# Late tokens in two and then four token tiles, v rows 140 slots behind the u rows

## The chip, the cores and the metric

One NeuronCore of a Trainium2 chip runs the whole kernel. The metric is the device time of one execution in microseconds, as the median of the runs. Everything is fp32. PE is the matmul engine, DVE the vector engine, ACT the scalar engine, POOL the engine that issues the indirect gathers, and SP the one whose queue issues the other DMAs.

## The reference, cut to what matters

One decoder layer over 1024 tokens of width 1024:

```
a = rms_norm(x, g);  z = a @ w_in                # 1024 x 4864: 38 column tiles of 128
z_rwkv, z_conv, z_gate = split(z)                # 14, 8 and 16 column tiles
z_rwkv = z_rwkv + (token_shift(z_rwkv) - z_rwkv) * mu
o_r = rwkv7(z_rwkv);  o_c = conformer_conv(z_conv)
h = x + (g_r * o_r + g_c * o_c) @ w_out          # g = sigmoid(z_gate)
c = rms_norm(h);  q = c @ w_q;  idx, gate = product_key_top16(q)    # 8 heads x 16 = 128 experts a token
coef = gate * gelu(sum_d(c * u_tab[idx]))        # u: 128 rows of 4 KB for each token
h = h + sum_e(coef * v_tab[idx])                 # v: 128 rows of 4 KB for each token
h = h + sigmoid(rms_norm(h) @ w_ple) * (p @ w_proj);  out = rms_norm(h)
```

For 1024 tokens the u rows and the v rows are 0.54 GB each. Each is read once.

## The kernel before

The tokens are eight tiles of 128 (`NT = 8`). Every engine runs a program written out by hand over positions (t, s): period t, slot s, with 128 slots in a period. In slot s of period t, DVE takes the dot product of c with the u row that expert column s gathered for the 128 tokens of tile t (`dot`). Also in period t each engine does, at fixed slots, its steps of `front` of tile t+1: the RWKV recurrence in slots 20 to 65, the convolution, the mixer products in slots 74 to 84, the query product and the top-k. So the order of the work is fixed on every engine, and an instruction that waits holds all that stands behind it on its engine.

**v rows.** `LAG = 2`: the v rows of tile t-2 are gathered and multiplied in period t. PE adds a gathered row, weighted, with four matmul records into `acc`. The u rows use five buffers (`UR`), the last of them `a_rstd`, and the v rows six (`VR`); once all u rows are done, the v rows use all eleven. POOL issues v row and u row in turn; a gather into a used buffer waits until that buffer's row has been used (`s_dot`, `s_vmm`). Periods 0 and 1 gather u rows alone, 2 to 7 both kinds, 8 and 9 v rows alone.

**The input projection.** The first 256 tokens are projected before period 0 (line 1170). The other 768 go in two blocks of 384 (`BEHIND_T`), one in period 0 and one in period 1 (line 1196): 38 column tiles of 8 products in each, at most four products in a slot, into the two halves of `acc`. A column tile's weights (512 KB) come into one of three buffers. ACT (lines 1411 to 1419) and DVE (`behind_out`) take it out of PSUM into one of two output buffers, halves of `e_hh`, and SP stores it to DRAM (`behind_store`), from where later periods read z, the convolution's input and the gates. The second block's normed x waits in DRAM and is read back at the start of period 1.

**The mixer weights** come through a ring of eight buffers of 256 KB, four of their own and four in `zb`, loaded from slots 40 and 66 on. `e_x` holds x of the next tile from slot 2 on; `e_hh` holds h of the tile whose v rows are being added.

**The end.** `tail` of a tile (the per-layer input gate, the last norm) runs in 20 slots; five tails run in period 7, one each in periods 8 and 9, and the last after them.

Of the kernel before, what the change touches and what calls it, by code (L numbers as in the profile page):

```python
# [122 lines left out]
UR, UW, VR, RING, RINGS = 5, 4, 6, 4, 8  # L123
# [17 lines left out]
AHEAD_T, BEHIND_T, BLOCKS = 2 * P, 3 * P, 2  # L141
W_Q_FIRST = (AHEAD_T + BEHIND_T) // P
# [7 lines left out]
LAG = 2  # L150
# [16 lines left out]
def v_place(m):  # L167

    alone = (NT - LAG) * NSEL
    if m < alone:  # L170
        return m % VR, m // VR + 1
    i, k = (m - alone) % (VR + UR), (m - alone) // (VR + UR) + 1
    return i, (alone // VR + k if i < VR else k)


def v_user(m):

    alone = (NT - LAG) * NSEL
    if m < alone:
        return m - VR if m >= VR else None  # L180
    if m - alone >= VR + UR:
        return m - VR - UR
    return m - VR if m - alone < VR else None
# [71 lines left out]
def block_of(n):  # L255

    return (n * P - AHEAD_T) // BEHIND_T if n * P >= AHEAD_T else None
# [7 lines left out]
def behind_weight(t, s):  # L265

    if not BEHIND_AT[t] <= s < BEHIND_END:
        return 0
    return 1 if HEAVY[0] <= s < HEAVY[1] and not FILLED[0] <= s < FILLED[1] else 3
# [8 lines left out]
def behind_products(t, s):  # L278

    done, total = (sum(behind_weight(t, i) for i in range(n)) for n in (s, SLOTS))  # L280
    first = 0 if t else AHEAD_COLS * KT
    n = COL_TILES * KT - first
    return range(first + n * done // total, first + n * (done + behind_weight(t, s)) // total)
# [7 lines left out]
def ring_slot(n, k):  # L291

    if k < RING:
        return 40 + k
    if k < RINGS:
        return MIX_AT + k - RING if n else FRONT_SLOTS
    return product_slot(k - RINGS)
# [13 lines left out]
def behind_done(t, s):  # L311

    if t == 0 and s < AHEAD_COLS:
        return [s]
    return [i // KT for i in behind_products(t, s) if i % KT == KT - 1]


def tail_step(t, s):

    if t == NT - 1:  # L320
        m, k = divmod(s - TAIL_AT, TAIL_SPAN)
        return (m, k) if 0 <= m < EARLY_TAILS else None
    if NT <= t < NT + LAG and 10 <= s < 10 + TAIL_SPAN:
        return EARLY_TAILS + t - NT, s - 10
    if t == NT + LAG and s < TAIL_SPAN:
        return NT - 1, s
    return None


def trunk(nc, io, dram):  # L330

    with ExitStack() as ctx:
# [15 lines left out]
        ring = [buf(f"e_ring{i}", [P, PAIRS, P]) for i in range(RING)]  # L348
# [3 lines left out]
        ring += [flat_zb[:, i * PAIRS * P:(i + 1) * PAIRS * P].rearrange("p (i t) -> p i t", i=PAIRS) for i in range(RINGS - RING)]  # L352
# [11 lines left out]
        z_r, z_k, z_v, lora = (zin[:, a:b, :] for a, b in ((0, 4), (4, 8), (8, 12), (12, 14)))  # L364
        p_w, p_run, p_dec, p_a = (part(a, 4, "p (i t) -> p i t", i=PAIRS) for a in (14, 18, 22, 26))
# [21 lines left out]
        blocks_at = KT * AHEAD_T  # L387
        behind = v_all[:, 0:3, :].rearrange("p a d -> p (a d)").rearrange("p (k t) -> p k t", k=KT)
        late = flat_q[:, blocks_at:blocks_at + KT * BEHIND_T].rearrange("p (k t) -> p k t", k=KT)
        w_a = [u[i][:, :].rearrange("p (k c) -> p k c", k=KT) for i in range(UW)]  # L390
        w_b = [v[3 + i].rearrange("p (k c) -> p k c", k=KT) for i in range(BW)]
        taken = blocks_at + KT * BEHIND_T
# [9 lines left out]
        b_zs, b_zq = wd[0][:, 0:BEHIND_T + 1], wd[1][:, 0:BEHIND_T]  # L402
        omm = buf("e_omm", [P, RWKV_TILES])
        b_cg = b_zq
        b_zo = [hh[:, i * HALF:i * HALF + BEHIND_T] for i in range(2)]
        z_last = buf("e_z_last", [P, RWKV_TILES])
        a_sq = [hh, gt]
        b_sum = a_rstd[:, AHEAD_T:]
        first_gates = [gt, hh]
# [24 lines left out]
        ps = psum("e_ps", [P, 2, HALF])  # L434
        c = psum("e_c", [P, D])
        pi = pd[:, :].rearrange("p (b t) -> p b t", b=2)
        idx_px, coef_px = ps[:, 0, 2 * NKEY:2 * NKEY + P], ps[:, 1, 2 * NKEY:2 * NKEY + P]

        s_const, s_iota = sem("e_constants"), sem("e_iota_made")
        s_w_q, s_w_tail = [sem(f"e_query_weights_in{i}") for i in range(2)], sem("e_tail_weights_in")  # L440
# [5 lines left out]
        s_late, s_lin = sem("b_late_tokens_stored"), [sem(f"b_late_tokens_in{i}") for i in range(PIECES)]  # L446
# [7 lines left out]
        s_bg = sem("b_mixer_gate_ready")  # L454
        s_bo, s_bst, s_wz = sem("b_output_ready"), [sem(f"b_output_stored{i}") for i in range(2)], sem("e_weights_cleared")
# [22 lines left out]
        s_u = [sem(f"e_u_in{i}") for i in range(UR)]  # L478
        s_v = [sem(f"e_v_in{i}") for i in range(VR + UR)]
# [20 lines left out]
        def tail_h(m):  # L500
            return hh if m == NT - 1 else xin

        @block.sync
        def _(sp):
            def stored(n, m):

                b, outs = block_of(n), stores_until(m)
                if b is None:
                    for i in range(2):
                        sp.wait_ge(s_ast[i], 16 * min(outs, outputs_until(COL_TILES)) // 2)  # L510
                    if outs > outputs_until(COL_TILES):
                        for i in range(2):
                            sp.wait_ge(s_agst[i], 16 * (outs - outputs_until(COL_TILES)) // 2)
                else:
                    for i in range(2):
                        sp.wait_ge(s_bst[i], 16 * (b * stores_until(COL_TILES) + outs) // 2)

            def rec_load(n):
                sp.wait_ge(s_y, n)
                stored(n, RWKV_TILES)  # L520
# [16 lines left out]
            def ring_load(n, which, m):  # L537
# [3 lines left out]
                elif k >= RING:  # L541
                    sp.wait_ge(s_rp, REC_PE * 2 * (n + 1))
                elif n:
                    sp.wait_ge(s_wu, 2 * KT * (n - 1) + k + RINGS + 1)
# [3 lines left out]
            def x_load(n):  # L548
                if n:
                    sp.wait_ge(s_sq, n)  # L550
                    sp.wait_ge(s_ctr, n)
                    sp.wait_ge(s_hout, 16 * n)
                sp.dma_start(xin[:, :], io["x"][n]).then_inc(s_xin, 16)
# [5 lines left out]
            def sum_load(n):  # L559
                sp.wait_ge(s_hout, 16 * (n + 1))  # L560
                if n:
                    sp.wait_ge(s_h2, 16 * n)
                else:
                    for i in range(2):
                        sp.wait_ge(s_bst[i], 16 * BLOCKS * stores_until(COL_TILES) // 2)
# [6 lines left out]
            def tail_loads(m):  # L572
                if m < NT - 1:
                    if m == 0:
                        sp.wait_ge(s_sq, NT)
                        sp.wait_ge(s_ctr, NT)
                        sp.wait_ge(s_hout, 16 * NT)
# [3 lines left out]
                    sp.dma_start(xin[:, :], dram["h2"][m]).then_inc(s_tin, 16)  # L581
# [14 lines left out]
            def front(n, s):  # L596
                if s == 2:
                    x_load(n)
# [10 lines left out]
                if s == MIX_AT + 14 and n + 1 < NT:  # L609
# [15 lines left out]
            def behind_w(b, m):  # L625
                i = b * COL_TILES + m
                if i >= BW:
                    sp.wait_ge(s_bm, i - BW + 1)
                sp.dma_start(w_b[i % BW], io["w_in"][column(m)]).then_inc(s_bw[i % BW], 16)

            def behind_store(b, m):
                i = stores_until(m)
                if kind(m) == "gate":
                    sp.wait_ge(s_bg, b * GATE_TILES + i + 1 - outputs_until(COL_TILES))
# [1546 lines left out]
```

## Time and profile before

| | us |
|---|---|
| median of 3 runs | 3628.08 (3624.88 to 3631.03) |
| span of the profiled execution, first to last instruction | 3429.3 |
| busy PE / DVE / POOL / ACT | 2702.1 / 2374.2 / 1976.9 / 525.9 |
| bytes moved, mean rate | 1249.58 MB, 364 GB/s |

The profiled execution's own device time is not recorded; its span is 198.8 us short of the median of the runs, and that difference is what lies around the span (launch, first loads of the program, end). A busy PE counts the modelled time of its matmuls, also where two run side by side. In the views of stretches each engine has its busy time and, in brackets, its instructions; PEclk is the granted TensorE clock as a share of 2.4 GHz (0.50 is 1.2 GHz); the DMA share can stand a little over 1.

### The profile page before, as it was taken

What the parts mean: (1) busy time and instruction counts of PE and PEld (TensorE: products, weight loads), DVE (VectorE), ACT (ScalarE), POOL (GpSimd) and SP (SyncE); (2) the same over time, 40 slices, a digit from 0 to 9 for tenths busy, and PEclk for the clock granted to TensorE, in tenths of its full rate; (3) what the DMA queues carried; (4) which work ended last, traced back from release to release, by engine and by line L of the source; (5) the groups of instructions that cost most, each with busy time, mean ns of one, the idle gap of its engine ahead of it and who ended that gap; (6) DMA issues with size and microseconds to landing.
All of it is one profiled execution on the core that took longest, in us unless ns stands there. A gap on an engine that the chain in (4) does not pass through costs nothing.

```text
span 3429.3 us, 41510 instructions
## 1 busy us (share of the span) xinstructions
PE 2702.1 (79%) x15300; PEld 1231.4 (36%) x15300; DVE 2374.2 (69%) x6064; ACT 525.9 (15%) x1165; POOL 1976.9 (58%) x2093
## 2 busy tenths in 40 slices
PE   9998998899766777787767767686777767778887
PEld 7775665565422322332233323232333112111111
DVE  5569888979898679877987798769875667520000
ACT  3223122212201011101110011002110111110001
POOL 1003344334577677767676767676766667757663
PEclk9999999999889987888798879887888789789999
DMA  6548899889999999999999999999999999999995
GB/s 211 184 156 284 297 354 335 283 288 344 361 400 406 401 409 409 407 394 406 407 408 401 397 407 408 405 395 409 408 404 404 409 407 407 409 369 393 401 362 237
DMA packets 380043, 1249.58 MB, mean 364 GB/s; under 512 B 40256, under 2 KB 76352, under 8 KB 379072
## 3 DMA queue, kind: packets, MB, share of 16 engines
q0 software_dynamic: 294912, 1073.87, 80.6%
q1 hardware_dynamic: 82624, 172.00, 14.2%
q8 instruction: 121, 1.98, 0.2%
q10 hardware_dynamic: 2304, 1.05, 0.1%
q14 instruction: 82, 0.67, 0.1%
HBM read 1217.27 MB, written 29.49 MB: 364 GB/s over the span
## 4 chain that ended last, share of the span: by engine, by line
DMA 27%; PE 13%; POOL 11%; DVE 10%; issue 5%; ACT 1%; SPq 0%; ACTq 0%; POOLq 0%
DMA e_u<-in_u_tab,e_idx 12%; DMA e_v<-in_v_tab,e_idxT 8%; POOL e_v L806 5%; PE e_acc L1126 5%; DMA e_a_rstd<-in_u_tab,e_idx 4%; POOL e_u L789 4%; DVE e_u L1972 3%; PE e_pd L1090 3%; PE e_pd L1011 2%; DMA e_u<-in_v_tab,e_idxT 1%; DMA e_x<-h_after_experts 1%; POOL e_a_rstd L789 1%; DVE e_a_rstd L1972 1%; DVE e_gbc L1709 1%; PE e_pd L928 1%
## 5 line engine op out<-in xcount | busy, mean ns | idle before, releaser
L1126 PE MATMUL e_acc<-e_v,e_wd 128*32 128x512 f32 x3636 | 1093.3, 719 | 463.6 <-DMA e_v<-in_v_tab,e_idxT 460.1
L789 POOL DMA_INDIRECT e_u<-in_u_tab,e_idx x820 | 797.5, 973 | 859.9 <-DVE e_dots L1972 487.1
L1972 DVE CUSTOM_DVE_ANT_0 e_u<-e_u,e_c 128x1024 f32<-128x1024 f32 x820 | 996.3, 1215 | 379.0 <-DMA e_u<-in_u_tab,e_idx 370.4
L806 POOL DMA_INDIRECT e_v<-in_v_tab,e_idxT x909 | 863.1, 950 | 334.2 <-issue 221.9
L1126 PEld LDWEIGHTS e_acc<-e_v,e_wd 128*32 128x32 f32 x3636 | 146.3, 116 | 1086.9 <-DMA e_v<-in_v_tab,e_idxT 901.6
L1196 PE MATMUL e_acc<-e_v 128*128 128x384 f32 x1216 | 435.5, 503 | 12.7 <-ACT e_wd L1413 11.2
L1972 DVE CUSTOM_DVE_ANT_0 e_a_rstd<-e_a_rstd,e_c 128x1024 f32<-128x1024 f32 x204 | 247.8, 1215 | 91.4 <-DMA e_a_rstd<-in_u_tab,e_idx 91.0
L1709 DVE SCALAR_TENSOR_TENSOR e_gbc<-e_hc,e_cw,e_gbc 128x128 f32<-128x128 f32 x960 | 307.8, 343 | 1.0
L789 POOL DMA_INDIRECT e_a_rstd<-in_u_tab,e_idx x204 | 198.6, 974 | 154.0 <-DVE e_dots L1972 123.9
L1196 PEld LDWEIGHTS e_acc<-e_v 128*128 128x128 f32 x1216 | 227.1, 195 | 162.8 <-issue 39.2
L831 PE MATMUL e_pd<-e_arena 64*64 64x64 f32 x3584 | 149.7, 233 | 52.0 <-DVE e_arena L1612 36.9
L1981 DVE TENSOR_TENSOR e_hh<-e_hh,e_acc 64x512 f32<-64x512 f32 (+1 forms) x24 | 16.4, 682 | 249.7 <-PE e_acc L1126 249.2
L831 PEld LDWEIGHTS e_pd<-e_arena 64*64 64x64 f32 x3584 | 127.0, 144 | 169.3 <-issue 74.1
L1260 ACT ACTIVATE e_arena<-e_pd 128x512 f32<-128x512 f32 (+1 forms) x192 | 90.4, 471 | 566.7 <-PE e_pd L831 373.7
L1011 PE MATMUL e_pd<-e_w_out,e_actT 128*128 128x512 f32 x256 | 134.1, 654 | 20.1 <-DVE e_actT L1846 20.1
L1170 PE MATMUL e_acc<-e_w_q,e_u 128*128 128x256 f32 x608 | 140.3, 386 | 3.4 <-DVE e_w_q L2057 3.4
L1037 PEld LDWEIGHTS e_pd<-e_actT,e_w_q 128*128 128x128 f32 x1024 | 126.4, 200 | 42.9 <-issue 37.5
L1037 PE MATMUL e_pd<-e_actT,e_w_q 128*128 128x128 f32 x1024 | 134.8, 288 | 0.3 <-ACT e_actT L1308 0.3
L1126 PE MATMUL e_acc<-e_u,e_wd 128*32 128x512 f32 x368 | 120.1, 602 | 18.2 <-DMA e_u<-in_v_tab,e_idxT 17.2
L1090 PE MATMUL e_pd<-e_w_out,e_actT 128*128 128x512 f32 x256 | 124.0, 618 | 2.3 <-ACT e_actT L1308 2.3
L1170 PEld LDWEIGHTS e_acc<-e_w_q,e_u 128*128 128x128 f32 x608 | 114.5, 192 | 21.7 <-issue 5.2
L806 POOL DMA_INDIRECT e_u<-in_v_tab,e_idxT x92 | 86.5, 940 | 46.4 <-issue 23.3
(272 smaller groups left out, 2695.3 us busy)
## 6 DMA issues: line engine op xcount, KB each, us to landing
e_v<-in_w_in SPq DMA_DIRECT2D x76, 512.0 KB, 6.3
e_u<-in_w_in SPq DMA_DIRECT2D x38, 512.0 KB, 3.8
e_v<-in_v_tab,e_idxT POOLq DMA_INDIRECT x909, 9.2
e_u<-in_u_tab,e_idx POOLq DMA_INDIRECT x820
e_ring<-in_w_c SPq DMA_DIRECT2D x32, 256.0 KB, 10.6
e_zb<-in_w_c SPq DMA_DIRECT2D x32, 256.0 KB, 7.7
e_ring<-in_w_r SPq DMA_DIRECT2D x32, 256.0 KB, 6.5
e_zb<-in_w_r SPq DMA_DIRECT2D x32, 256.0 KB, 8.1
```

What stands on the lines that cost most here:

```text
L789: pool.indirect_dma_start(out=u[m % UR][:, :], out_offset=None, in_=io["u_tab"], in_offset=bass.IndirectOffsetOnAxis(ap=idx[n % 2][:, j:j ...
L806: pool.indirect_dma_start(out=v[i], out_offset=None, in_=io["v_tab"], in_offset=bass.IndirectOffsetOnAxis(ap=idxT[n % (LAG + 1)][:, k:k + ...
L831: last = pe.matmul(pi[r, out, i * CH:(i + 1) * CH], a[r, i, :], b[r, i, :] if len(b.shape) == 3 else b[r, :], start=True, stop=True)
L1011: last = pe.matmul(pd[:, h * HALF:(h + 1) * HALF], mixt[:, k, :], w_out[:, k, h * HALF:(h + 1) * HALF], start=(k == 0), stop=(k == KT - 1))
L1037: last = pe.matmul(pd[:, h * P:(h + 1) * P], w_q[:, k, h * P:(h + 1) * P], actT[:, k, :], start=(k == 0), stop=(k == KT - 1))
L1090: last = pe.matmul(pd[:, h * HALF:(h + 1) * HALF], actT[:, k, :], w_ple[:, k, h * HALF:(h + 1) * HALF], start=(k == 0), stop=(k == KT - 1))
L1126: last = pe.matmul(acc[rows, cols], w[:, at_:at_ + 32], v[v_place(m)[0]][:, cols], start=(step == 0), stop=True, skip_group_check=True)
L1170: last = pe.matmul(out, w_a[m % UW][:, k, :], ahead[:, k, :], start=(k == 0), stop=(k == KT - 1))
L1196: last = pe.matmul(acc[:, m % 2 * HALF:m % 2 * HALF + BEHIND_T], w_b[n % BW][:, k, :], behind[:, k, :], start=(k == 0), stop=(k == KT - 1))
L1260: act.activation(dst, src, ACT.Copy).then_inc(s_ra, 1)
L1709: dve.scalar_tensor_tensor(out=out, in0=hc[:, i, j:j + P], scalar=col(cw, j * CONV_TILES + i), in1=out, op0=ALU.mult, op1=ALU.add).then_in ...
L1972: dve.tensor_tensor_reduce(u[m % UR][:, :], u[m % UR][:, :], c[:, :], 1.0, 0.0, ALU.mult, ALU.add, dots[n % 2][:, j:j + 1]).then_inc(s_dot, 1)
```

## The change

- Periods 0 and 1: the block of period 0 is now 256 tokens (two tiles). The other 512 tokens (four tiles) are a block of their own in slots 130 to 300, counted from the start of period 0 (period 1 and the first 45 slots of period 2), with two or three products of 512 tokens in a slot and none in the slots of the mixer products.
- The late block has one PSUM bank of its own, `pl`, one weight buffer in two halves of 256 KB (4 of 8 products each), and one pair `l_zs`, `l_zo` in a new buffer `side`. Its x stays in SBUF, in four buffers that later hold rows.
- v rows follow the u rows by 140 slots (`V_LAG`), not by 256. The u rows have 4 buffers and the v rows 4 until slot 312; then 6 and 7; after the last u row the v rows have all 13.
- The mixer weights' ring has 12 buffers, all in memory of the recurrence, all loaded from slot 66 of a period on. `hh` and `xin` are one buffer; `x_load` moves to slot 30, `sum_load` to slot 112. Six tails run in period 7.

```diff
-UR, UW, VR, RING, RINGS = 5, 4, 6, 4, 8
+UW, VW, LW, RINGS = 4, 5, 4, 12
-AHEAD_T, BEHIND_T, BLOCKS = 2 * P, 3 * P, 2
+AHEAD_T, BEHIND_T, LATE_T = 2 * P, 2 * P, 4 * P
-BEHIND_AT, BEHIND_END, PIECES = (2, 4), 124, 4
+BEHIND_AT, BEHIND_END = 2, 120
-LAG = 2
+V_HEAD = 12
+LAG, V_LAG = 1, NSEL + V_HEAD
+CHUNKS = 2
+MORE_AT = 2 * SLOTS + 56
+U_FIRST, V_FIRST = list(range(UW)), list(range(UW, UW + VW - 1))
+U_LATER = U_FIRST + [UW + VW, UW + VW + 1]
+V_LATER = V_FIRST + [UW + VW - 1, UW + VW + 2, UW + VW + 3]
...
+def late_room(s):
+    if HEAVY[0] <= s < FILLED[0] or FILLED[1] <= s < MIX_AT + 32 or MIX_AT + 38 <= s < MIX_AT + 48:
+        return 0
+    return 3 if 10 <= s < REC_AT or s >= MIX_AT + 48 else 2
+def late_slots():
+    at_, g, i = {}, SLOTS + 2, 0
+    first = g
+    while i < COL_TILES * KT:
+        room = late_room(g % SLOTS) if g >= first else 0
+        n = min(room, KT - i % KT)
+        at_[g] = range(i, i + n)
+        i += n
+        if n and i % KT == 0:
+            first = g + 1
+        g += 1
+    return at_
...
             def ring_load(n, which, m):
                 k = which * KT + m
                 if k >= RINGS:
                     sp.wait_ge(s_wu, 2 * KT * n + k - RINGS + 1)
-                elif k >= RING:
+                else:
                     sp.wait_ge(s_rp, REC_PE * 2 * (n + 1))
+                if k == RINGS - 1:
+                    sp.wait_ge(s_rv, REC_DVE * 2 * (n + 1))
...
+            def late_w(q):                                            # SP
+                m, half = divmod(q, CHUNKS)
+                if q >= CHUNKS:
+                    sp.wait_ge(s_lu, q - CHUNKS + 1)
+                sp.dma_start(w_late[:, half, :, :], io["w_in"][column(m)][:, k, :]).then_inc(s_lw[half], 16)
...
+                    for q in late_chunks_done(t, s):                  # SP, in slot s
+                        if q + CHUNKS < CHUNKS * COL_TILES:
+                            late_w(q + CHUNKS)
+                    for m in late_done(t, s, 2):
+                        if kind(m) != "conv gate":
+                            late_store(m)
...
+            def late_product(i):                                      # PE
+                m, k = divmod(i, KT)
+                half, in_half = divmod(k, KT // 2)
+                if k == 0 and m:
+                    pe.wait_ge(s_lf, m)
+                if in_half == 0:
+                    pe.wait_ge(s_lw[half], 16 * (m + 1))
+                last = pe.matmul(pl[:, :], w_late[:, half, in_half, :], late[:, k, :], start=(k == 0), stop=(k == KT - 1))
+                if in_half == KT // 2 - 1:
+                    last.then_inc(s_lu, 1)
...
+            def late_out(m):                                          # ACT; DVE adds l_zs to l_zo a slot later
+                act.wait_ge(s_lu, CHUNKS * (m + 1))
+                i = stores_until(m)
+                    act.wait_ge(s_lst, 16 * i)
+                if kind(m) == "z":
+                    act.activation(l_zs[:, 0:1], col(z_last, column(m)), ACT.Copy)
+                    act.activation(l_zs[:, 1:], pl[:, :], ACT.Copy, scale=col(vec, COL["mu"] + column(m)))
+                    act.activation(l_zo, pl[:, :], ACT.Copy, scale=col(omm, column(m))).then_inc(s_lf, 1)
+                if kind(m) == "gate":
+                    act.activation(l_zo, pl[:, :], ACT.Sigmoid).then_inc(s_lf, 1)
```

## Rows read from the trace of the kernel before

**Rows 1.** Stretches by period: engines' busy time, clock, DMA share, GB/s.
```profile
core 0: us, PE busy (x) PEld busy (x) DVE busy (x) ACT busy (x) POOL busy (x), PEclk, DMA share, GB/s
0.00:257.00 257.00, 239.17 (x1749) 195.17 (x1749) 148.59 (x415) 67.39 (x155) 10.24 (x45) 0.99 0.55 183
257.00:578.00 321.00, 291.56 (x1700) 185.28 (x1699) 281.18 (x742) 73.75 (x151) 126.18 (x131) 0.95 0.91 315
578.00:905.00 327.00, 302.05 (x1732) 192.56 (x1733) 287.23 (x750) 77.95 (x161) 124.57 (x130) 0.96 0.91 311
905.00:1261.00 356.00, 257.16 (x1637) 102.61 (x1636) 283.30 (x730) 43.56 (x101) 251.33 (x262) 0.85 1.02 403
...
2687.00:3023.00 336.00, 247.47 (x770) 64.67 (x770) 217.40 (x506) 50.34 (x111) 237.46 (x249) 0.81 1.03 408
3023.00:3205.00 182.00, 149.93 (x550) 31.97 (x549) 12.44 (x21) 14.38 (x37) 120.38 (x128) 0.97 0.98 383
3205.00:3390.00 185.00, 154.12 (x572) 33.25 (x571) 6.42 (x10) 10.69 (x31) 120.46 (x128) 0.98 0.98 383
```

**Rows 2.** Stretches inside period 1 (slots 0-7, 40-47) and period 3 (slots 0-7).
```profile
580.00:605.00 25.00, 22.41 (x80) 14.27 (x81) 24.83 (x56) 12.96 (x27) 7.93 (x8) 0.85 0.91 331
...
715.00:739.00 24.00, 24.00 (x218) 14.87 (x217) 18.29 (x53) 3.63 (x7) 7.97 (x9) 1.00 0.85 280
...
1263.00:1291.00 28.00, 15.94 (x66) 5.62 (x65) 24.52 (x55) 10.44 (x21) 16.81 (x17) 0.81 1.03 409
```

**Rows 3.** Waits (total, times, longest, us): periods 2 to 6.
```profile
PE e_acc L1126 <- DMA e_v<-in_v_tab,e_idxT: 372.3, 316, 8.8
...
DVE e_u L1972 <- DMA e_u<-in_u_tab,e_idx: 284.3, 305, 8.8
```

**Rows 4.** Waits: period 0.
```profile
POOL e_u L789 <- DVE e_dots L1972: 159.8, 98, 5.9
...
DVE e_u L1972 <- DMA e_u<-in_u_tab,e_idx: 6.7, 6, 1.7
```

**Rows 5.** Timeline of PE: start, us, group; 256, 384 and 512 columns, one v row.
```profile
109.03 1.99 PE L1170 MATMUL e_acc<-e_w_q,e_u 128*128 128x256 f32 x8
...
678.30 4.14 PE L1196 MATMUL e_acc<-e_v 128*128 128x384 f32 x12
...
1003.20 1.05 PE L1126 MATMUL e_acc<-e_v,e_wd 128*32 128x512 f32 x4
...
3064.68 7.13 PE L1090 MATMUL e_pd<-e_w_out,e_actT 128*128 128x512 f32 x16
```

**Rows 6.** Groups of PE (busy, mean ns, idle before), periods 1 and 2.
```profile
L1196 PE MATMUL e_acc<-e_v 128*128 128x384 f32 x608 | 217.5, 503 | 7.4 <-ACT e_wd L1413 6.6 <-ACT e_hh L1419 0.7
...
L1126 PE MATMUL e_acc<-e_v,e_wd 128*32 128x512 f32 x512 | 154.1, 733 | 73.3 <-DMA e_v<-in_v_tab,e_idxT 73.0
```

**Rows 7.** DMA of period 1: queue's share; issues with KB and us to landing.
```profile
q1 hardware_dynamic: 22439, 34.98, 32.1%
...
mixer_gates<-e_hh SPq DMA_DIRECT2D x17, 192.0 KB, 5.5
shifted_projection<-e_hh SPq DMA_DIRECT2D x14, 192.0 KB, 7.8
```

**Rows 8.** DMA of period 2, the same.
```profile
q1 hardware_dynamic: 3692, 8.04, 6.1%
...
e_zb<-in_w_c SPq DMA_DIRECT2D x4, 256.0 KB, 7.7
```

**Rows 9.** DMA of period 0: its gate stores.
```profile
mixer_gates<-e_hh SPq DMA_DIRECT2D x15, 192.0 KB, 9.1
```

**Rows 10.** Groups of ACT by shape: copies out of PSUM, a table load.
```profile
L1260 ACT ACTIVATE e_arena<-e_pd 128x512 f32<-128x512 f32 x80 | 47.8, 597 | 360.5 <-PE e_pd L831 214.2 <-PE e_pd L858 144.8 <-issue 1.5
...
L1411 ACT ACTIVATE e_wd<-e_z_last 128x1 f32<-128x1 f32 x28 | 5.7, 202 | 99.2 <-DVE e_hh L1789 52.8 <-PE e_acc L1196 46.3
...
L1419 ACT ACT_TABLE_LOAD x7 | 9.0, 1283 | 9.2 <-DMA mixer_gates<-e_hh 9.1
```

More of the change, by code:

```diff
@@ L164, in strip_of, with gather_rows, take, v_at @@
     return lane ^ (2 * h)
[L167 to L183, printed above, removed]
+MORE_AT = 2 * SLOTS + 56
+U_FIRST, V_FIRST = list(range(UW)), list(range(UW, UW + VW - 1))
+U_LATER = U_FIRST + [UW + VW, UW + VW + 1]
+V_LATER = V_FIRST + [UW + VW - 1, UW + VW + 2, UW + VW + 3]
+def gather_rows():
+    free_from, turns, held = [-1] * (UW + VW + LW), [0] * (UW + VW + LW), [None] * (UW + VW + LW)
+    u_rows, v_rows = [], []
+    def take(g, among, kind, m, rows):
+        i = min(among, key=lambda b: free_from[b])
+        turns[i] += 1
+        rows.append((i, turns[i], held[i]))
+        free_from[i], held[i] = g, (kind, m)
+    for g in range(NT * SLOTS + V_LAG):
+        if g >= V_LAG:
+            among = V_FIRST if g < MORE_AT else V_LATER if g < NT * SLOTS else V_LATER + U_LATER
+            take(g, among, "v", g - V_LAG, v_rows)
+        if g < NT * SLOTS:
+            take(g, U_FIRST if g < MORE_AT else U_LATER, "u", g, u_rows)
+    return u_rows, v_rows
+U_ROWS, V_ROWS = gather_rows()
+def v_at(t, s):
+    q = t * SLOTS + s - V_LAG
+    return divmod(q, NSEL) if 0 <= q < NT * NSEL else None
 def head_slot(h):
@@ L364, in trunk @@
         z_r, z_k, z_v, lora = (zin[:, a:b, :] for a, b in ((0, 4), (4, 8), (8, 12), (12, 14)))
+        ring = [flat_zb[:, i * PAIRS * P:(i + 1) * PAIRS * P].rearrange("p (i t) -> p i t", i=PAIRS) for i in range(6)]
+        ring += [part(a, 4, "p (i t) -> p i t", i=PAIRS) for a in (0, 4, 8, 22, 26, 30)]
         p_w, p_run, p_dec, p_a = (part(a, 4, "p (i t) -> p i t", i=PAIRS) for a in (14, 18, 22, 26))
@@ L608, in front @@
                     h_store(n)
[L609 removed]
+                if s == MIX_AT + 18 and n + 1 < NT:
                     rec_load(n + 1)
@@ L650, in _, with late_store @@
+            def late_store(m):
+                if kind(m) == "z":
+                    sp.wait_ge(s_lo, m + 1)
+                else:
+                    sp.wait_ge(s_lf, m + 1)
+                block_store(1, m, l_zo, s_lst)
             for k in range(KT):
@@ L654, in _ @@
                 ahead_w(m)
-            for b, x in enumerate((behind, late)):
-                first = AHEAD_T + b * BEHIND_T
-                sp.dma_start(x, io["xT"][:, :, first:first + BEHIND_T].rearrange("k p t -> p k t")).then_inc(s_bx, 16)
+            for x, (first, size) in zip((behind, late), BLOCKS):
+                sp.dma_start(x, io["xT"][:, :, first:first + size].rearrange("k p t -> p k t")).then_inc(s_bx, 16)
             sp.dma_start(cw[:, :], io["dw_w"]).then_inc(s_up, 16)
@@ L779, in _, with row_free @@
             pool.tensor_copy(iot[:, :], ioti[:, :]).then_inc(s_iota, 1)
+            for i in range(2):
+                pool.memset(wd[i][:, :], 0.0).then_inc(s_iota, 1)
+            def row_free(i, held):
+                if held:
+                    pool.wait_ge({"u": s_dot, "v": s_vmm}[held[0]], held[1] + 1)
+                elif i >= UW + VW - 1:
+                    pool.wait_ge(s_lu, CHUNKS * COL_TILES)
+                elif i >= UW:
+                    pool.wait_ge(s_bm, COL_TILES)
             def gather_u(n, j):
-                m = n * NSEL + j
+                i, turn, held = U_ROWS[n * NSEL + j]
@@ L809, in _ @@
-            for t in range(NT + LAG):
-                for j in range(NSEL):
-                    if t >= LAG:
-                        gather_v(t - LAG, j)
+                row_free(i, held)
+                pool.indirect_dma_start(out=rows_in[i], out_offset=None, in_=io["v_tab"],
+                                        in_offset=bass.IndirectOffsetOnAxis(ap=idxT[n % (LAG + 1)][:, k:k + 1], axis=0)).then_inc(s_row[i], 16)
+            for t in range(NT + LAG + 1):
+                for s in range(SLOTS):
+                    if v_at(t, s):
+                        gather_v(*v_at(t, s))
@@ L1125, in add_tokens @@
                         at_ = (step % QUARTER) * P + 32 * lane
-                        last = pe.matmul(acc[rows, cols], w[:, at_:at_ + 32], v[v_place(m)[0]][:, cols], start=(step == 0), stop=True,
+                        last = pe.matmul(acc[rows, cols], w[:, at_:at_ + 32], rows_in[row][:, cols], start=(step == 0), stop=True,
                                          skip_group_check=True)
@@ L1393, in block_square @@
                 into = a_sq[k % 2] if k else b_sum
-                for b, x in enumerate((behind, late)):
-                    act.activation(into[:, b * BEHIND_T:(b + 1) * BEHIND_T], x[:, k, :], ACT.Square).then_inc(s_bsq, 1)
+                for x, cols in zip((behind, late), BLOCK_COLS):
+                    act.activation(into[:, cols], x[:, k, :], ACT.Square).then_inc(s_bsq, 1)
             def block_root():
```

434 lines of the change are left out of this document (218 added, 216 removed).

## The prediction

> **What bounds the kernel now.** I read the stretches by period first [rows 1]. Periods 2 to 7 take 2118 us for 768 slots (905 to 3023), 2.76 us a slot, and the DMA share there is 1.02 to 1.03 at 403 to 408 GB/s: the row traffic is the bound. The waits of these periods agree: both PE and DVE wait for rows, 372 and 284 us [rows 3]. Periods 0 and 1 are another regime. They gather half as many rows in 321 and 327 us, at a DMA share of 0.91 and 315 GB/s; PE is busy for 92% of them. Inside period 1 the bound changes with the slot: in slots 0 to 7 DVE is busy 24.8 of 25 us, in slots 40 to 47 PE 24.0 of 24.0 us [rows 2]. Periods 8 and 9, with v rows alone, take 367 us for 256 rows, 1.43 us a row.
>
> So the bytes hardly change, and what there is to win is DMA time left unused: in period 1 about 327 x (1.03 - 0.91) / 1.03 = 38 us, as much in period 0, which the change doesn't fill with v rows, and some 16 us where v rows come alone (1.43 us a slot against 2.76 / 2 = 1.38, and loads of the tails). The change starts v rows 116 slots earlier, in the time of the old period 1.
>
> **Prologue and period 0.** The first 257 us keep their work; twelve ring loads at slot 66 instead of four early ones might add up to 5 us, the dropped store of x takes some away: 0 (bounds -5 and +5). In period 0 the products shrink from 384 to 256 columns. Eight records took 1.99 us with 256 columns and twelve 4.14 us with 384 [rows 5], 0.25 and 0.345 us each with the last one's tail, so 608 records [rows 6] lose about 60 us of PE: 292 - 60 = 232 us of 321. DVE, with 281 us busy, is left as the bound. It cannot be under 281 us, and at most nothing is won, 321 us; slots where DVE is full show it can run near its busy time [rows 2], so I take 281 x 1.06 = 298 us.
>
> The u rows have four buffers here, not five. A row now holds a buffer 5 x 2.51 = 12.5 us, but DVE waited for rows only 6.7 us in the whole period, while POOL waited 160 us for free buffers [rows 4]: rows lie ready. Four buffers at 298 / 128 = 2.33 us give 9.3 us. I price it at 0; were the whole 12.5 us needed, it would be 128 x 3.1 = 400 us.
>
> **Slots 128 to 303, the late stage.** Three floors.
>
> DMA: 176 slots x 2.76 = 486 us for rows and `front`. (In 12 of these slots no v row comes; there DVE, as in rows 2, holds the slot at about 3 us, so I leave nothing off.) The column tiles add to it. The SP queue's share was 32.1% of 327 us = 105 us in period 1 [rows 7] and 6.1% of 356 us = 22 us in period 2 [rows 8]; the difference over 38 tiles is 2.2 us, and with 256 KB stored instead of 192 KB about 2.3 us a tile. 38 x 2.3 = 87 us, less the four conv gate tiles' missing stores, gives 572 us.
>
> PE: sixteen records of 512 columns took 7.13 us, 0.446 each [rows 5], so 608 records are 271 us. A v row is 1.05 us [rows 5]; 164 of them are 172 us (somewhat less, since the end of one overlaps what follows). The rest of period 2 on PE, 257 - 154 [rows 1, 6] = 103 us or 0.80 us a slot, is 141 us for 176 slots. Sum 584 us, barely above DMA's 572. DVE's floor is lower: 284 us a period is 390 us.
>
> The hand-over of a column tile is the third. `pl` and `l_zo` are single. PE's first product of tile m+1 waits for ACT's copy of tile m; that copy waits until the store of tile m-1 has landed; and SP issues the store of tile m-1 behind its wait for the first weight half of tile m to be used up. So per stored tile one chain closes: ACT's copies 0.20 + 2 x 0.60 [rows 10] and 0.1 of semaphores, 1.5 us; four products 8 x 0.446 = 3.6 us, and because they lie in two slots one v row and half a slot of `front` between them, 1.0 + 0.4 us; then the store. Its landing took 7.8 us in period 1 and for gates between 5.5 and 9.1 us [rows 7, 9], for 192 KB. For 256 KB under a full DMA queue I take 8.0 us; the bounds are 5.5 and, from these rows, 9.1 (a 256 KB load in period 2 took 7.7 [rows 8]). Sum 14.5 us a stored tile. For gates ACT has one copy, but sometimes a table load of 1.28 us [rows 10]; I keep 14.5. Behind a PE that waits here stand the v products and the recurrence, so POOL's gathers stop too: four v buffers are four slots.
>
> From the schedule: the 14 z tiles have 57 slots (130 to 186), the 8 conv tiles 57 (187 to 243), the 16 gate tiles 57 (244 to 300). z: DMA floor 57 x 2.76 + 14 x 2.3 = 189, chain 14 x 14.5 = 203 us, the chain is later. Gates: 57 x 2.76 + 16 x 2.3 = 194 against 16 x 14.5 = 232 us, the chain again. Conv: half of them store nothing, and their slots hold the mixer products: 57 x 2.76 + 18 = 175 us by DMA. Remaining 5 slots 14 us. Sum 203 + 175 + 232 + 14 = 624 us.
>
> The weights' halves are not late in this: a half is asked for once used and needed about a chain later, at least 8 us, against 7.7 us of landing [rows 8]. Were they late, the cost would lie in the same tiles.
>
> The Trainium skill, in Trainium Kernel Development and Optimization, Best Practices, asks for double buffers so that DMA and compute overlap; this change goes the other way for PSUM, output and weights at once. By that rule the chain binds in every stored tile, as I have it. The old block had two of each, and in period 1 PE waited for ACT's copies only 7.4 us [rows 6].
>
> **Slots 304 to 1023.** 720 slots x 2.76 = 1987 us. Row buffers are now 6 and 7, not 5 and 6. The rate was 403 to 408 GB/s where single stretches reach 409 [rows 1, 2]: at most 1%, 20 us, at least 0; I take 6. The move of the v tile's change from slot 0 to slot 12 takes a hand-over out of the slots where DVE is fullest; both ways under 2 us a period, 0. `x_load` and `sum_load` stay far ahead of their users (slot 30 for slot 98, slot 112 for slot 12); the ring at slot 66 has 8 slots, 22 us, for 3 MB, 8 us at the full rate: 0, and some 5 us a period if SP is held up there. 1981 us.
>
> **The end.** 140 v rows x 1.43 = 201 us, and 3429.3 - 3390 = 39 us for the last tail [rows 1]. Six tails in period 7 are covered: DVE is busy 217 of 336 us there.
>
> **Sum.** 257 + 298 + 624 + 1981 + 201 + 39 = 3400 us, 29 less than the span of 3429.3. The median of the runs is 198.8 us above that span; what lies around it doesn't change. 3628 - 29 = 3599 us.
>
> **Rivals.**
> - *The chain is hidden.* If stores land in 6 to 7 us, a stored tile's chain is 12.5 to 13.5 us, under the 13.6 us that a tile's slots need; then PE's floor of 584 us holds the late stage: 3360 us, 3559 in all. For it: 5.5 us for the gates of period 1 [rows 7]. Against it: 7.8 us for z, and that queue was less full than now. The Trainium skill, DMA: Bandwidth & Descriptors, in its fit of a DMA's time, puts it at about 2.0 us plus bytes at 436 GB/s, an estimate of 2.6 us for such a store; by that rule the chain would be 9.1 us and this case the outcome. The rows of landings speak against it.
> - *The chain is longer, and the change loses.* Place: the same wait of ACT for the store. Break-even: the late stage may take 653 us; less 189 for the rest that is 464 us for 30 stored tiles, 15.5 us each, a landing of 9.0 us. The gate stores of period 0 took 9.1 us [rows 9]. With 10.5 us of landing, or with recurrence steps that come late behind the blocked PE, 17 us a tile, the stage takes 699 us: 3475 us, 3674 in all.
> - *Four u buffers are too few.* If a row's round trip is over 9.3 us, period 0 stays at 321 us or above and the late stage, where a slot is over 3.3 us, doesn't notice: 3423 us at least, 3622.
>
> **Chances.** Forecast 0.43, chain hidden 0.22, chain longer 0.29, u rows short 0.06. The median can be told from no change beyond about 0.2%, 7 us. The forecast's own range is 3580 to 3625, three quarters of it faster by more than that, the rest near no change; with 0.21 of the hidden chain that makes faster 0.53, same 0.13 (0.08 of the forecast, 0.04 of the short u rows, 0.01), slower 0.34. The range takes in both chain cases: 3550 to 3680.
>
> **What would show it.** Period 0 near 298 us with POOL's waits for `e_dots` smaller. In slots 130 to 186 and 244 to 300: ACT waiting for DMA `shifted_projection<-e_side` and `mixer_gates<-e_side`, PE's late products waiting for ACT, starts of the stored tiles 14 to 15 us apart, a DMA share under 1.0. Without these waits the first rival holds; with tiles 16 us or more apart the second. After slot 304, 2.75 us a slot. I am wrong beyond the chain if the steady slot changes: if the later x and ring loads hold up the mixer, or seven and six buffers raise the rate above 409 GB/s.

## The result and the profile after

The changed kernel is slower: 3649.2 us median of 15 runs against 3633.5 us for the kernel before, ratio 1.0042 with a 95% interval of 1.0026 to 1.0057, some 15 us. Beside the kernel before on another occasion it gave 1.0029 (1.0013 to 1.0046). I had forecast 3599 us, 29 us faster.

First a correction that concerns every absolute number of the forecast. The profiled execution of the kernel before had a span of 3429 us, and I took the 199 us to the median for what lies around the span. It is not that: an execution of which both are recorded has a device time only 1.7 us over its span (3654.27 and 3652.5 us, the changed kernel). That one execution ran at another rate of row traffic. Profiled again, the same kernel has a span of 3649 us, with 371 GB/s in its steady stage where the first trace had 404. The 220 us between the two spans all lie in the stages with v rows; periods 0 and 1 are alike (644 us in the second trace, 648 in the first). So I compare with this second trace, `e1_before_again`.

By stage, with cuts at the first dot product, at dots 128, 304 and the last, and at the last v row. The kernel before, second trace:

```profile
core 0: us, PE busy (x) PEld busy (x) DVE busy (x) ACT busy (x) POOL busy (x), PEclk, DMA share, GB/s
0.00:261.00 261.00, 240.76 (x1760) 195.75 (x1760) 152.30 (x435) 72.03 (x162) 13.55 (x48) 1.00 0.55 186
261.00:575.00 314.00, 287.59 (x1693) 183.25 (x1693) 277.75 (x725) 70.62 (x146) 124.10 (x128) 0.96 0.92 320
575.00:1059.00 484.00, 398.08 (x2392) 230.65 (x2392) 403.66 (x1058) 97.81 (x205) 223.21 (x230) 0.87 0.92 324
1059.00:3228.00 2169.00, 1475.33 (x8289) 581.43 (x8287) 1509.35 (x3815) 252.19 (x570) 1375.89 (x1435) 0.79 0.98 371
3228.00:3616.00 388.00, 307.48 (x1122) 66.36 (x1122) 13.16 (x23) 23.75 (x66) 238.92 (x254) 0.96 0.94 357
3616.00:3650.00 34.00, 20.27 (x49) 8.96 (x48) 6.73 (x12) 8.71 (x18) 0.00 (x0) 0.81 0.04 15
```

The changed kernel, the same stages; they answer to [rows 1]:

```profile
0.00:265.00 265.00, 242.85 (x1762) 200.19 (x1762) 152.03 (x435) 71.76 (x162) 13.47 (x49) 0.98 0.53 177
265.00:588.00 323.00, 240.71 (x1691) 193.26 (x1692) 276.19 (x725) 68.34 (x150) 123.82 (x128) 0.87 0.86 301
588.00:1256.00 668.00, 599.45 (x2893) 238.42 (x2891) 414.45 (x1061) 102.50 (x220) 327.14 (x342) 0.95 0.90 325
1256.00:3416.00 2160.00, 1476.87 (x8302) 620.57 (x8301) 1509.91 (x3823) 259.08 (x584) 1383.45 (x1440) 0.77 0.98 375
3416.00:3621.00 205.00, 166.14 (x610) 36.10 (x608) 6.72 (x11) 12.52 (x36) 126.09 (x134) 0.95 0.95 365
3621.00:3653.00 32.00, 18.55 (x49) 8.34 (x48) 6.74 (x12) 8.70 (x18) 0.00 (x0) 0.86 0.04 17
```

Two stages lose, one wins. Period 0 takes 323 us where the kernel before took 314, though PE is 47 us less busy in it; its DMA share fell from 0.92 to 0.86. Slots 128 to 303 take 668 us against 484, with PE busy for 90% and a DMA share of 0.90: the row traffic is below the 0.98 that it reaches from slot 304 on, so it does not bind all of that stage. The stage of v rows alone shrinks from 388 to 205 us. The 720 slots between are alike (2160 and 2169 us).

The hand-over of a late tile stands in the timeline of the changed kernel as a chain (start, us, then the group; in brackets the idle time before it):

```profile
705.81 0.20 ACT L1518 ACTIVATE e_side<-e_z_last 128x1 f32<-128x1 f32 x1 [10.10 <-DMA shifted_projection<-e_side]
705.92 0.67 ACT L1519 ACTIVATE e_side<-e_pl,e_vec 128x512 f32<-128x512 f32 x1
706.49 0.68 ACT L1520 ACTIVATE e_side<-e_pl,e_omm 128x512 f32<-128x512 f32 x1
...
707.22 1.99 PE L1284 MATMUL e_pl<-e_late,e_v 128*128 128x512 f32 x4 [1.12 <-ACT e_side L1520]
...
710.12 1.98 PE L1284 MATMUL e_pl<-e_late,e_v 128*128 128x512 f32 x4
...
712.51 0.43 SPq L708 DMA_DIRECT2D shifted_projection<-e_side  x1
...
723.05 0.20 ACT L1518 ACTIVATE e_side<-e_z_last 128x1 f32<-128x1 f32 x1 [4.30 <-DMA shifted_projection<-e_side]
```

ACT waits 10.1 us for a store to land, copies for 1.4 us, PE may start the next tile at 707.2, is through with four products at 712.1, and only then does SP issue the store of the tile copied at 707.2. It lands 10.5 us later, at 723.05. The totals over slots 128 to 303 are among the waits of the changed kernel (engine, line, total, times, longest):

```profile
POOL e_v L885 <- PE e_acc L1207: 244.2, 127, 16.1
ACT e_side L1524 <- DMA mixer_gates<-e_side: 93.9, 10, 15.6
ACT e_side L1518 <- DMA shifted_projection<-e_side: 81.4, 9, 18.1
...
PE e_pl L1284 <- ACT e_side L1520: 26.6, 12, 8.1
...
PE e_pl L1284 <- DMA e_v<-in_w_in: 14.9, 4, 12.8
```

By the first line POOL stands 244 us before v gathers because PE has not used the rows. Not all of that is the hand-over's: 191 us are left in e3_store_early, where the hand-over waits are nearly gone.

### The profile page after: what moved, and what is told of

Read it like the earlier page. It is cut to its first block, busy times and chain, and to the rows that moved or that the text cites. A ratio compares the mean times of both kernels' runs of the same rounds, so it can differ in the third digit from the quotient of the medians.

```text
span 3652.5 us, 41502 instructions
## 1 busy us (share of the span) xinstructions
PE 2744.6 (75%) x15300; PEld 1296.9 (36%) x15300; DVE 2366.0 (65%) x6065; ACT 522.9 (14%) x1167; POOL 1974.0 (54%) x2093
## 4 chain that ended last, share of the span: by engine, by line
PE 31%; DVE 21%; DMA 15%; another core or an unknown queue 13%; issue 12%; POOL 5%; ACT 3%; SPq 1%; POOLq 0%; ACTq 0%; DVEq 0%
PE e_acc L1207 8%; DVE e_u L2082 7%; DMA e_u<-in_u_tab,e_idx 5%; PE e_pl L1284 5%; PE e_acc L1251 3%; PE e_pd L1116 3%; PE e_pd L910 2%; DVE e_late L2082 2%; DMA e_v<-in_v_tab,e_idxT 2%; DMA mixer_gates<-e_side 2%; DMA shifted_projection<-e_side 2%; PE e_pd L1170 2%; DVE e_gbc L1816 2%; PE e_pd L1090 2%
## 5 line engine op out<-in xcount | busy, mean ns | idle before, releaser
L885 POOL DMA_INDIRECT e_v<-in_v_tab,e_idxT x734 | 697.1, 950 | 634.1 <-PE e_acc L1207 369.5
L1207 PE MATMUL e_acc<-e_v,e_wd 128*32 128x512 f32 x2936 | 846.9, 715 | 215.3 <-DMA e_v<-in_v_tab,e_idxT 138.1
L1207 PE MATMUL e_acc<-e_late,e_wd 128*32 128x512 f32 x992 | 308.6, 736 | 72.8 <-DMA e_late<-in_v_tab,e_idxT 48.6
L1284 PE MATMUL e_pl<-e_late,e_v 128*128 128x512 f32 x608 | 310.7, 639 | 58.5 <-ACT e_side L1520 26.6
L2082 DVE CUSTOM_DVE_ANT_0 e_late<-e_late,e_c 128x1024 f32<-128x1024 f32 x238 | 289.4, 1216 | 99.3 <-DMA e_late<-in_u_tab,e_idx 60.8
L885 POOL DMA_INDIRECT e_late<-in_v_tab,e_idxT x248 | 234.7, 946 | 156.4 <-PE e_acc L1207 63.1
L877 POOL DMA_INDIRECT e_late<-in_u_tab,e_idx x238 | 230.8, 970 | 94.2 <-issue 66.9
L1272 PE MATMUL e_acc<-e_v 128*128 128x256 f32 x608 | 157.3, 406 | 18.9 <-ACT e_side L1507 10.2
L1090 PE MATMUL e_pd<-e_w_out,e_actT 128*128 128x512 f32 x256 | 135.2, 658 | 29.7 <-DVE e_actT L1955 23.8
L1272 PEld LDWEIGHTS e_acc<-e_v 128*128 128x128 f32 x608 | 118.3, 203 | 45.1 <-issue 28.1
```

The costliest lines, as they stand in the source:

```text
L877: pool.indirect_dma_start(out=rows_in[i], out_offset=None, in_=io["u_tab"], in_offset=bass.IndirectOffsetOnAxis(ap=idx[n % 2][:, j:j + 1], ...
L885: pool.indirect_dma_start(out=rows_in[i], out_offset=None, in_=io["v_tab"], in_offset=bass.IndirectOffsetOnAxis(ap=idxT[n % (LAG + 1)][:, ...
L1090: last = pe.matmul(pd[:, h * HALF:(h + 1) * HALF], mixt[:, k, :], w_out[:, k, h * HALF:(h + 1) * HALF], start=(k == 0), stop=(k == KT - 1))
L1207: last = pe.matmul(acc[rows, cols], w[:, at_:at_ + 32], rows_in[row][:, cols], start=(step == 0), stop=True, skip_group_check=True)
L1272: last = pe.matmul(acc[:, m % 2 * HALF:m % 2 * HALF + BEHIND_T], w_b[m % BW][:, k, :], behind[:, k, :], start=(k == 0), stop=(k == KT - 1))
L1284: last = pe.matmul(pl[:, :], w_late[:, half, in_half, :], late[:, k, :], start=(k == 0), stop=(k == KT - 1))
```

## The experiments

Each ratio is to the kernel before, run on the same chip.

**e1_before_again.** The kernel before, no edit.

> The kernel before, unchanged, profiled on the chip on which the others of this call run. The first profiled execution had a span of 3429 us while its timed runs took 3633 us, and the profiled execution of the changed kernel had 3652 us; so the two traces are not at one rate. If the chip's row traffic is simply slower in most executions, periods 3 to 6 take about 380 to 390 us each here (355 in the first trace), the DMA rate in them is near 370 GB/s, and the span is near 3630 us. If instead the changed kernel's later periods are slower by its own doing (390 us each), they take about 355 us here and the missing 200 us lie somewhere else. Ratio to the kernel before 1.000.

Ratio 1.0002 (0.9986 to 1.0018). Periods 3 to 6 take 391.5 us each (356.5 in the first trace). The two traces differ in rate, and the changed kernel's later periods (390.1 us) are not slower by its own doing.

**e2_changed_again.** The changed kernel, no edit.

> The changed kernel, unchanged, beside the kernel before on one chip: ratio 1.002 to 1.006. Theory A (the hand-over of a late column tile: PE waits for ACT's copy, ACT for the landing of the store before, SP issues that store only behind the next weight half): slots 128 to 303 take 650 us or more, over 60 us more than the kernel before needs for its second block and 48 steady slots minus what is saved; periods 3 to 6 equal those of the kernel before within 5 us each. Rival B (the steady periods are worse: the later x load and the ring at slot 66, or the 13 buffers): periods 3 to 6 are 5 us or more longer each than in the kernel before on this chip.

Ratio 1.0029 (1.0013 to 1.0046). Slots 128 to 303 take 669 us, periods 3 to 6 392.9 us each. Rival B is out: later x loads, the ring at slot 66 and 13 buffers for 11 change nothing in the steady stage when taken together. The run can't tell them apart, so a small gain of one may hide a small cost of another.

**e3_store_early.** The late tile's store ahead of the next weight half, and in the slot after the tile is done instead of two slots after.

```diff
+                    for m in late_done(t, s, 1):
+                        if kind(m) != "conv gate":
+                            late_store(m)
                     for q in late_chunks_done(t, s):
                         if q + CHUNKS < CHUNKS * COL_TILES:
                             late_w(q + CHUNKS)
-                    for m in late_done(t, s, 2):
-                        if kind(m) != "conv gate":
-                            late_store(m)
```

> The changed kernel with one edit on SP: a late column tile is stored in the slot after it is done and ahead of the wait for the next weight half, not two slots after and behind it. Theory A: the store no longer waits for four products of the next tile; 4 to 5 us leave each of 30 chains, of which the part over the slots' own time (about 3 to 4 us a tile) is won, so slots 128 to 303 shrink by 60 to 110 us, ACT's waits for shifted_projection<-e_side and mixer_gates<-e_side (63 and 64 us) nearly vanish, and the ratio to the kernel before is 0.97 to 0.99. Rival C (four and four row buffers, or PE's own load, bound the late stage): under 20 us are won, ratio 1.000 to 1.005.

Ratio 0.9935 (0.9912 to 0.9958). The place of one store in SP's program is worth 36 us of the median. Slots 128 to 303 fall from 669 to 625 us. The waits of that stretch:

```profile
POOL e_v L885 <- PE e_acc L1207: 191.2, 107, 16.4
ACT e_side L1524 <- PE e_pl L1284: 104.6, 16, 12.0
...
PE e_pl L1284 <- DMA e_v<-in_w_in: 17.6, 7, 13.0
...
ACT e_side L1518 <- DMA shifted_projection<-e_side: 3.7, 1, 3.7
```

ACT now waits for PE, as it should, and hardly for stores. The theory of the hand-over stands: the wait goes when the store's issue moves, with no other work changed. It goes although `pl` and `l_zo` are still single: the chain needed the late store as well as the single buffers. The stage won 44 us, less than the 60 to 110 I expected, and what is left is a PE busy for 581 of 624 us and one wait of 13 us for a weight half.

**e4_ring_spread.** On top of e3, the ring loads two a slot.

```diff
-    return MIX_AT if k < RINGS else product_slot(k - RINGS)
+    return MIX_AT + k // 2 if k < RINGS else product_slot(k - RINGS)
```

> The kernel of e3_store_early with the twelve ring loads of a period two a slot in slots 66 to 71, not all in slot 66. Theory: in period 1 PE stood 13 us for a weight half that was queued behind 3 MB of ring loads; spread out they let it through. Then PE's wait for e_v<-in_w_in (17.6 us in slots 128 to 303) falls under 6 us, slots 128 to 303 shrink by 8 to 13 us from 625, the ratio to the kernel before is 0.989 to 0.992 (e3: 0.9935). Rival: those 13 us are made up anyway, since the rows' traffic goes on meanwhile; ratio as e3 within 0.002.

Ratio 0.9900 (0.9877 to 0.9923). The one wait of 13 us is gone (the longest is now 2.9 us), but the total is not under the 6 us that I expected:

```profile
PE e_pl L1284 <- DMA e_v<-in_w_in: 12.8, 9, 2.9
```

The stage took 619 us, 6 less, where I had expected 8 to 13. The intervals of this ratio and of 0.9935 overlap, so the runs alone do not tell e4 from e3; that the wait vanished is shown, what it was worth is 6 us by one trace of each.

**e5_rows_in_pairs.** On top of e3, two v rows at a time.

```diff
-TOGETHER, LAST_TOGETHER = 1, 4
+TOGETHER, LAST_TOGETHER = 2, 4
```

> The kernel of e3_store_early with TOGETHER = 2: PE adds two v rows at a time, on four strips of the array, so that two rows cost it about 0.9 us and not 1.8 us. Theory: once the store comes early, PE's own work is the bound of slots 128 to 303 (busy 576 of 619 us); it loses about 70 us of work there, and the stage goes to its DMA floor, 600 to 610 us instead of 625: ratio 0.986 to 0.991. Rival (four v buffers bind): with rows used in pairs, two of four buffers are held for a partner, POOL waits longer for PE and the stage gets no shorter or grows by 10 us and more; ratio 0.994 or above. In the steady periods, where rows are the bound, no change is expected by either (390 us).

Ratio 1.0088 (1.0067 to 1.0109). The stage stayed at 625 us, and the steady periods, where I had expected no change, grew from 391.9 to 404.4 us each. The stretches: slots 128 to 303, and periods 3 to 6.

```profile
586.00:1211.00 625.00, 527.37 (x2864) 234.16 (x2865) 414.64 (x1061) 102.97 (x220) 328.18 (x341) 0.94 0.95 348
...
1460.00:3074.00 1614.00, 991.61 (x6538) 488.71 (x6537) 1118.57 (x2884) 176.15 (x405) 985.77 (x1025) 0.72 0.95 356
```

PE lost 53 us of busy time in the first, and none of it came back as time. The likely reason is that a row that waits for its partner holds a buffer; in that stage POOL stood before v gathers for 175.5 us in 61 waits, 191.2 us in 107 in e3, so each wait was longer. No run shows this as the cause, nor why the steady periods grew. This alone doesn't say which of PE's work and the buffers bound e3, since the edit changed both in opposite ways. e9 tests PE's work by itself.

**e6_half_first_block.** The changed kernel with half of the products of period 0 left out (it computes something else).

```diff
+                if 1 <= k <= 4:
+                    return
                 last = pe.matmul(acc[:, m % 2 * HALF:m % 2 * HALF + BEHIND_T], w_b[m % BW][:, k, :], behind[:, k, :],
```

> The changed kernel with four of the eight products of each column tile of period 0 left out (k = 1 to 4), so the projections of tokens 256 to 511 are sums over half of the width. PE loses 65 us of work in period 0. Question: why period 0 did not get shorter than 321 us though its products shrank by a third (325 us measured). If PE still counted there, period 0 falls to 305 us or less. If DVE's program or the four u buffers set it, it stays within 5 us of 322 us.

Period 0 took 317 us, with PE busy for 198 us of it, and the kernel's ratio was 1.0052 (1.0032 to 1.0071), no better than the changed kernel's. Complete products gave 323, 324 and 318 us (the changed kernel twice and e3, whose edit does not touch period 0), so one trace can be off by some 6 us, and 317 shows no gain. PE's products do not bound period 0 any more.

**e7_before_four_u.** The kernel before with four u buffers.

```diff
-UR, UW, VR, RING, RINGS = 5, 4, 6, 4, 8
+UR, UW, VR, RING, RINGS = 4, 4, 6, 4, 8
```

> The kernel before with four u buffers instead of five (UR = 4), nothing else. If the fifth u buffer is what period 0 of the changed kernel misses, periods 0 and 1 are 5 us or more longer each here than in e1_before_again (316.5 and 325.3 us), and DVE waits over 20 us for u rows in period 0 instead of 7. If four are enough, as forecast, both stay within 3 us. Steady periods, ten buffers instead of eleven: if the row traffic needs the depth, over 395 us a period, else 392.

Ratio 1.0205 (1.0177 to 1.0232), 75 us for one buffer of 4 KB a partition. Period 0 went from 314 to 326 us, period 1 from 330 to 336, each steady period from 391.5 to 404.8. These differences of traces are somewhat large, since this profiled execution was the slowest of its five and that of e1_before_again the fastest of its ten: the spans differ by 96 us, the medians by some 75. DVE's waits for u rows in period 0, first in e1_before_again, where `a_rstd` is the fifth buffer, then here:

```profile
DVE e_u L1972 <- DMA e_u<-in_u_tab,e_idx: 5.0, 3, 2.5
DVE e_a_rstd L1972 <- DMA e_a_rstd<-in_u_tab,e_idx: 2.8, 2, 2.0
```

```profile
POOL e_u L789 <- DVE e_dots L1972: 194.6, 116, 5.2
DVE e_u L1972 <- DMA e_u<-in_u_tab,e_idx: 22.7, 17, 3.7
```

The changed kernel has the second picture in its period 0:

```profile
POOL e_u L877 <- DVE e_dots L2082: 189.1, 118, 10.4
...
DVE e_u L2082 <- DMA e_u<-in_u_tab,e_idx: 24.3, 19, 3.7
```

**e8_fifth_u_buffer.** On top of e4, two weight buffers for the block of period 0, and the third as a fifth u buffer in that period.

```diff
-BW = 3
+BW = 2
...
-            take(g, U_FIRST if g < MORE_AT else U_LATER, "u", g, u_rows)
+            take(g, U_FIRST + [UW] if g < SLOTS else U_FIRST if g < MORE_AT else U_LATER, "u", g, u_rows)
...
-        w_b = [v[:, i, :].rearrange("p (k c) -> p k c", k=KT) for i in (3, 4, 0)]
+        w_b = [v[:, i, :].rearrange("p (k c) -> p k c", k=KT) for i in (3, 4)]
...
```

> The kernel of e4_ring_spread with two weight buffers instead of three for the block of period 0, and the freed one as a fifth u buffer in that period only. Theory: four u buffers cost period 0 what the lighter products gave it (the kernel before with four lost 12 us in period 0, 10 us in period 1). Then period 0 falls from 317 to 325 us to 300 to 308 us, DVE's wait for u rows in it from about 24 us to under 10 us, and the ratio to the kernel before is 0.985 to 0.988 (e4: 0.990). Rival: DVE's program alone sets period 0 (281 us busy and its own dependent waits); it stays at 315 us or more and the ratio stays at 0.990. A third way: weights that now arrive with less lead hold PE, over 10 us of waits for e_v<-in_w_in in period 0.

Ratio 0.9869 (0.9848 to 0.9890), the fastest complete kernel of this study: 1.3% under the kernel before. The interval overlaps that of e4 (0.9877 to 0.9923), so what the buffer gave is read from period 0. It took 315 us in e4, on which this run is built, and 302 us here; first e4, then this run:

```profile
264.00:579.00 315.00, 237.54 (x1692) 190.58 (x1693) 276.04 (x726) 68.86 (x152) 124.10 (x128) 0.88 0.89 309
```

```profile
264.00:566.00 302.00, 240.23 (x1692) 189.43 (x1693) 275.34 (x726) 69.03 (x152) 122.62 (x127) 0.91 0.91 325
```

The waits in period 0, first e4's, then this run's:

```profile
DVE e_u L2082 <- DMA e_u<-in_u_tab,e_idx: 28.8, 24, 3.4
```

```profile
PE e_acc L1270 <- DMA e_v<-in_w_in: 26.2, 16, 5.6
...
DVE e_u L2080 <- DMA e_u<-in_u_tab,e_idx: 4.2, 4, 1.8
```

DVE's wait for rows fell from 28.8 us in e4 (24.3 in the changed kernel) to 4.2 us, and the period is 13 us shorter. The third way came as well, 26 us of PE's waits for weights, but PE had the room.

**e9_half_late_products.** On top of e4, half of the late products left out (it computes something else).

```diff
                 if in_half == 0:
                     pe.wait_ge(s_lw[half], 16 * (m + 1))
+                if in_half in (1, 2):
+                    return
```

> The kernel of e4_ring_spread with half of the late products left out (two of four in each weight half), so z, convolution input and gates of tokens 512 to 1023 are sums over half of the width; loads, copies and stores stay. PE loses 135 us of work in slots 128 to 303 (618 us). If PE's work is what binds the stage now, it falls to its DMA floor, under 600 us. If the four and four row buffers bind it, as e5_rows_in_pairs suggests, which took 70 us of PE work away and won nothing, it stays over 608 us and POOL's waits for e_acc and e_dots stay too.

Ratio 0.978 (0.976 to 0.9799), from two runs. The stage, first in e4_ring_spread, then here:

```profile
579.00:1197.00 618.00, 582.62 (x2888) 233.10 (x2886) 413.99 (x1059) 102.59 (x218) 325.45 (x342) 0.98 0.96 350
```

```profile
576.00:1159.00 583.00, 481.07 (x2585) 179.66 (x2585) 415.58 (x1061) 102.47 (x218) 327.70 (x342) 0.92 0.98 372
```

It falls by 35 us for 102 us less of busy PE, and the DMA share reaches 0.98, that of the steady stage. So in e4 PE's work binds for at least 35 us, with the same four and four buffers. That 583 us is what the row traffic needs is my reading of the 0.98; no run took the buffers as the only change in this stage.

## Why the prediction was wrong

The forecast as differences, against the mean of the changed kernel's two traces less the kernel before's second (by the stages above; the forecast's own cuts lie up to some 5 us elsewhere, so its terms add up to -31 here and to -29 there):

| term | forecast | measured |
|---|---|---|
| prologue | 0 | +3 |
| period 0 | -23 | +9 |
| slots 128 to 303 | +164 | +184 |
| 720 steady slots | -6 | +2 |
| v rows alone | -166 | -182 |
| sum | -31 | +16 |

The forecast's +164 is 624 us less the 460 us that the first trace has for these slots; 166 is 367 less 201; 0 for the tail.

**Period 0: the step that failed.** "Four buffers ... I price it at 0." Measured, a fifth u buffer is worth 12 to 13 us of period 0: taking it away costs 12 us in the kernel before (e7), and giving it back takes e4's 315 us to 302 (e8), near the 298 us of the forecast. I had the right two numbers, 12.5 us a buffer held and 9.3 us with four, and read from DVE's 6.7 us of waiting [rows 4] that rows lie ready. That sum left out the fifth buffer's own line, so with five buffers DVE waited 8.8 us in all:

```profile
DVE e_a_rstd L1972 <- DMA e_a_rstd<-in_u_tab,e_idx: 2.1, 2, 1.6
```

More important, rows that lie ready on the average say little of single rows. I worked out from the completion records of e1_before_again when each row of slots 8 to 125 of period 0 had landed: 6.8 us after the start of its gather on the average, but between 4.2 and 10.5 us. It then lay ready for 4.0 us. With four buffers (e7) the landing takes the same, 6.5 us, and the row lies ready for only 2.1 us; DVE started its dot product within 0.3 us of the landing, so had in all likelihood waited for it, 28 times of 118 and not 15. The changed kernel has 6.6, 2.0 and 31. With the dot product's 1.2 us the mean round trip with four buffers was 7.7 us, under the 9.3 us that they give, and the buffer was needed for the scatter around the mean.

The rival with four u buffers was there, with 0.06, and its period 0 "at 321 us or above" is what came; but its condition, a round trip over 9.3 us, holds only for the late rows. That PE would stop being the bound was right (e6). Of the 32 us that this term is off, 7 are the base (I counted from 321 us, the second trace has 314), 13 are the buffer by e8, and 4 are the rest of 302 over 298. The remaining 8, between 323 us here and 315 in e4, are as large as the scatter between traces and the spread ring loads together and stay open.

**Slots 128 to 303: right mechanism, 20 us short.** The stage took 668 us and not 624, but the kernel before also took 24 us more for these slots than in its first trace (484 and 460). The chain runs as forecast, and its parts were off both ways. In the timeline above it is 1.4 us of copies and 5.3 us from the start of the next tile's products to the store's issue (1.5 and 5.0 forecast). Over the 14 z tiles of that trace, from the first copy to the store's issue took 8.0 us on the average, between 6.7 and 11.8, where I had 6.5; the landing took 7.2 us on the average, where I had 8.0 (over all stores of the stage but the last a median of 6.9, from 4.8 to 11.8). So the landing was sized too long, and the time between copy and issue, in which PE does its four products and what stands between them, too short.

By PE's first products the 14 z tiles took 218 us (203 forecast), the 16 gate tiles 229 (232) and the conv tiles 214 where I had 175. In the conv tiles' slots the row rate is lower than in the first trace, 3.05 us a slot in periods 3 to 6 and not 2.76, an estimate of 57 x 0.29 = 17 us, if the rate binds there (DMA share 0.94). One weight half queued behind 3 MB of ring loads at slot 66 held PE for 13 us, and its removal in e4 shortened the stage by 6. The rest of these 39 us stays open. I had said "0, and some 5 us a period if SP is held up"; the loads did cost something, once, because the late block's weights share their queue. That the chain is real is shown by e3. The break-even I gave, 15.5 us a stored tile, was met by the z tiles (218 / 14 = 15.6) and not by the gates (14.3). In the differences of the table this term alone turns -31 into -11 us; with period 0 as forecast the change would still have been a small gain.

**v rows alone and the steady stage.** 116 v rows went from a stage of 1.52 us a row (1.43 forecast) into one with u rows: 182 us, 16 more than forecast; v rows alone are slower in the second trace, as the steady stage is. The steady stage shows no gain from 13 buffers; I took 6 us from a range of 0 to 20, and its lower end was right.

**The time.** 3649 us lies in the range I gave (3550 to 3680), on the side to which I gave 0.34. The 199 us that I had explained wrongly do not enter the difference, but every term was priced at the rate of the fast execution. That the misses of the late stage (+20) and of the v rows alone (-16) nearly cancel is luck. Of the 47 us that the sum of differences is off, 32 are in the term of period 0.

The Trainium skill's advice to double-buffer so that DMA and compute overlap (Trainium Kernel Development and Optimization, Best Practices) fits the waits of the changed kernel, whose output is single; but e3 removed them without a second buffer, and e7 shows that the fifth of five buffers was still worth 2%. The fit for one DMA's time in the Trainium skill (DMA: Bandwidth & Descriptors, Anatomy of one DMA) is given there for DMAs issued from GpSimd. The estimate of 2.6 us that I took from it does not describe these stores from SP beside row traffic: they took 4.8 to 11.8 us.

## What to carry to other kernels

Count a buffer by the late rows and by the longest stretch in which its user is busy elsewhere, not by how seldom the user waits on the average: here 4.0 us of lying ready were the reserve, and half of it was too little. Where an output buffer is single, look at the issuing queue's program order: a store behind a wait for the next tile's progress makes a chain out of two things that could overlap, and moving that store was worth 36 us here. And before pricing from a profile, see that its span and the runs' times belong together; here a gap of 5% was another rate, not overhead.

## What the runs showed of the hardware

The same program's row gathers ran at 404 GB/s with a DMA share of 1.02 in one execution and at 371 GB/s with 0.98 in another. Every timed run of the kernel before, 3623 us and more, fits the second and not the first (span 3429 us); what sets the rate stays open. A load can be late through what its own queue holds: in the changed kernel PE waited 12.8 us for a weight half issued right behind the twelve ring loads, and no more than 2.9 us once e4 had spread them. SP's issue of such a load stayed short: in e3_store_early 1.6 us for that one, 0.33 to 0.51 us for the other 75. One store some 10 us behind took 4.3 us to issue, where most take 0.4; no run shows why.
